# Hybrid encoder step on one core: order of loads, copies and sums around the MLP's down projection

## What is computed

```python
x = x + out                                   # attention output times w_o
h = rmsnorm(x, norm_mlp[i])
x = x + jnp.square(jax.nn.relu(h @ mlp_w_up[i])) @ mlp_w_down[i]   # hidden 4096
```

## Time and profile before

| | us |
|---|---|
| median of 3 runs | 2820.52 |
| profiled execution, device time | 2818.45 |
| its span | 2816.5 |
| PE busy | 2679.4 (95%) |
| PE weight loads busy | 2247.5 (80%) |
| DVE busy | 1735.6 (62%) |
| ACT busy | 1157.7 (41%) |
| POOL busy | 739.1 (26%) |

### The profile page before, as it was taken

One profiled execution on the slowest core, in us unless ns is written; L12 is line 12 of the kernel. 1 busy time (PEld: TensorE's weight loads), 2 busy tenths in 40 slices (PEclk: granted clock), 3 DMA queues, 4 the chain that ended last, 5 costly groups with the idle time before them and its releaser, 6 DMA issues. The chain is left out here.

```text
span 2816.5 us, 40390 instructions
## 1 busy us (share of the span) xinstructions
PE 2679.4 (95%) x14531; PEld 2247.5 (80%) x14531; DVE 1735.6 (62%) x2325; ACT 1157.7 (41%) x2260; POOL 739.1 (26%) x633
## 2 busy tenths in 40 slices
PE   7989998899999989999699999998999999999998
PEld 6878887778888878888598886776888888778886
DVE  5656665266555678888311007887485555688887
ACT  4334445243333333333312218998343333333333
POOL 3100001135544400000312115665145544300001
PEclk9999999899999999999899999999999999999999
DMA  4311113514444564533134537773324444644342
GB/s 147 87 59 46 43 52 105 187 60 145 139 135 142 186 221 132 161 128 109 62 126 146 157 109 180 173 172 113 121 91 150 135 137 141 241 159 161 123 157 101
DMA packets 285845, 368.81 MB, mean 131 GB/s; under 512 B 25952, under 2 KB 205664, under 8 KB 285664
## 3 DMA queue, kind: packets, MB, share of 16 engines
q1 hardware_dynamic: 285664, 366.42, 40.8%
HBM read 242.19 MB, written 124.16 MB: 130 GB/s over the span
## 5 line engine op out<-in xcount | busy, mean ns | idle before, releaser
L2291 DVE TENSOR_TENSOR x<-m_ps,x 128x1024 f32<-128x1024 f32 x224 | 273.1, 1219 | 98.9 <-PE m_ps L76 98.9
L2008 POOL TENSOR_TENSOR m_u<-m_u,m_u 128x512 f32<-128x512 f32 x128 | 175.8, 1384 | 340.3 <-DVE m_u L2138 335.2
L1954 POOL TENSOR_SCALAR m_stat<-m_stat 128x1 f32<-128x1 f32 x36 | 11.9, 329 | 862.2 <-ACT m_sqjunk L1901 693.8
L2126 DVE TENSOR_TENSOR m_z<-m_ps,m_part 128x512 f32<-128x512 f32 x96 | 66.3, 690 | 143.9 <-PE m_ps L76 142.0
L1759 ACT COPY m_part<-m_ps 128x512 f32<-128x512 f32 x96 | 56.4, 588 | 197.4 <-PE m_ps L76 197.4
L2114 DVE TENSOR_TENSOR m_up<-m_upr,m_up 128x512 fp32r<-128x512 f32 x128 | 87.8, 706 | 28.5 <-ACT m_up L1746 28.5
L3237 ACT ACTIVATE e_b<-e_ps 128x512 f32<-128x512 f32 (+3 forms) x192 | 95.9, 500 | 12.0 <-PE e_ps L3433 11.4
L76 PE MATMUL m_ps<-m_t1h,m_up 128*128 128x512 f32 x256 | 99.7, 390 | 0.0
L74 PE MATMUL m_ps<-m_t1h,m_up 128*128 128x512 f32 x256 | 99.6, 389 | 0.0
L75 PE MATMUL m_ps<-m_t1l,m_up 128*128 128x512 f32 x256 | 99.6, 389 | 0.0
L1746 ACT CAST m_up<-m_upr 128x512 fp32r<-128x512 f32 x128 | 75.7, 616 | 57.2 <-PE m_ps L76 57.2
(11 more groups left out here) (1175 smaller groups left out, 9093.9 us busy)
## 6 DMA issues: line engine op xcount, KB each, us to landing
scratch_u<-m_u SPq DMA_DIRECT2D x224, 256.0 KB, 2.2
m_ur<-scratch_u SPq DMA_DIRECT2D x208, 256.0 KB, 2.7
m_upr<-in_mlp_w_up SPq DMA_DIRECT2D x32, 1024.0 KB, 5.9
m_wr<-in_mlp_w_down SPq DMA_DIRECT2D x64, 512.0 KB, 6.9
scratch_x<-x SPq DMA_DIRECT2D x18, 512.0 KB, 2.6
x<-scratch_x SPq DMA_DIRECT2D x4, 2048.0 KB, 11.4
scratch_qr<-a_qrst SPq DMA_DIRECT2D x9, 512.0 KB, 3.4
a_x<-in_x_prompt SPq DMA_DIRECT2D x8, 512.0 KB, 4.9
```

The costliest lines, as they stand in the source:

```text
L2008: pool.tensor_tensor(u_st[out][:], u_st[a][:], u_st[b][:], op).then_inc(u_summed.sem, 1)
L2291: dve.tensor_tensor(out, bank[:, at:at + 2, :], out, ALU.add).then_inc(summed.sem, 1)
```

## The change

All edits are inside `output_and_mlp_stage`, for both layers. In words:

1. SP, first chunk: all seven operands of pass 0 and A11 of pass 1 are loaded in one run, then u of the last pair and the sample part of the pair before are stored, and only then comes x. x returns in five pieces (two tiles each, and the sample tile) where there were three; pieces for tiles 2, 3 and 6, 7 are issued after the weights of chunk 1. The other six operands of pass 1 are issued right after the last up product, ahead of weights "21" and "22" of chunk 1 and of the last stores; before they came after the wait for B12's low part. `load_tokens` now also waits for the low part of the buffer's last user from the ninth operand on.
2. Last up pair: ACT's third `keep_part` stands before the copies of T2, T1; DVE's second `join` and `activate` stand before the low parts of T2, T1. The sum T3 moves from POOL to DVE; T4's sum moves back behind the token parts. ACT copies S4 before B22.
3. First up pair: the weight sums S1 and S2 of pair 0 move from POOL to DVE (`first_up_sums`), between the low part of A12 and the rest of the last row tile's parts; the four pieces of T4 are copied after S2 and S1 in one run.
4. Last pass: ACT squares rows 0, 1 and the sample tile before it copies S4 and A22 of the last pass, and in layer 0 also scales two tiles before A22. POOL makes the roots of three rows before it multiplies two tiles by the gain, then two more roots, then three multiplications.

```diff
@@ SP
-                if m >= 16:
+                if m >= 8:
                     before, j = divmod(m - 8, 7)
                     sp.wait_ge(tok_lo[TOKEN_OPERANDS[j]].sem, before + 1)
...
             sp.wait_ge(up_lo.sem, UP_STEPS * PAIRS_FF)
-            load_tokens(0, "A11")
-            load_tokens(0, "A12")
-            load_tokens(0, "S2")
+            for n in TOKEN_OPERANDS:
+                load_tokens(0, n)
+            load_tokens(1, "A11")
+            store_u(LAST, 0)
+            store_sample_u(LAST - 1)
...
-                tiles = (slice(0, 4), slice(4, 8), slice(8, 9))[i]
+                tiles = (slice(0, 2), slice(2, 4), slice(4, 6), slice(6, 8), slice(8, 9))[i]
...
             sp.wait_ge(prod.sem, up_done(LAST, "P6"))
             reload_x(0)
-            store_u(LAST, 0)
-            for n in ("S1", "S3", "S4", "A22"):
-                load_tokens(0, n)
-            load_tokens(1, "A11")
             sp.wait_ge(prod.sem, up_done(LAST, "P7"))
-            reload_x(1)
             store_u(LAST, 1)
-            store_sample_u(LAST - 1)
+            reload_x(2)
             sp.wait_ge(prod.sem, up_done(LAST, "P4"))
             load_sample_tokens(0)
             store_u(LAST, 2)
             sp.wait_ge(prod.sem, up_done(LAST, "P3"))
+            for n in TOKEN_OPERANDS[1:]:
+                load_tokens(1, n)
             load_weights(1, "21")
             load_weights(1, "22")
             store_u_sums(LAST)
@@ (store_sample_u(LAST) and the wait for five low parts stay here)
             load_weights(1, "11")
             load_weights(1, "12")
-            for n in TOKEN_OPERANDS[1:]:
-                if n == "A22":
-                    sp.wait_ge(u_out[6].sem, 16 * PAIRS_FF)
-                load_tokens(1, n)
+            reload_x(1)
+            reload_x(3)
             u_stored(PAIRS_FF)
-            reload_x(2)
+            reload_x(4)
             load_sample_tokens(1)
@@ ACT, up pairs
                 if p == 0:
-                    fourth_features_hi((0, 1))
                     up_operand_hi("S2", 0)
                     up_operand_hi("S1", 0)
-                    fourth_features_hi((2, 3))
+                    fourth_features_hi((0, 1, 2, 3))
...
-                if not more:
-                    weight_hi(0, "T2")
-                    weight_hi(0, "T1")
...
                 keep_part(p, 2)
...
                 if not more:
-                    weight_hi(0, "T3")
+                    weight_hi(0, "T2")
+                    weight_hi(0, "T1")
                     token_hi(0, "A11")
...
                 else:
+                    weight_hi(0, "T3")
                     token_hi(0, "A12")
                     token_hi(0, "S2")
...
             copy_sample(PAIRS_FF - 1)
+            token_hi(0, "S4")
             weight_hi(0, "B22")
-            token_hi(0, "S4")
@@ ACT, last pass
+            for i in range(3):
+                squares_2(i)
+            token_hi(LAST_G, "S4")
             if final:
-                for i in range(NT):
+                token_hi(LAST_G, "A22")
+                for i in range(3, NT):
                     squares_2(i)
             else:
-                for i in range(3):
-                    squares_2(i)
                 scale_early(0)
                 scale_early(1)
+                token_hi(LAST_G, "A22")
                 squares_2(3)
@@ POOL
-            up_sums(0, ("S1", "S2"))
             inverse_rms(NPT, stat, squared, mean, rs)
             up_sums(0, ("S3", "S4"))
...
-            pool.wait_ge(*weight_in(0, "22"))
-            pool.wait_ge(prod.sem, up_done(PAIRS_FF - 1, "P5"))
-            pool.tensor_tensor(sum_t3[:], wt_raw[0]["22"][:], wt_raw[0]["12"][:], ALU.subtract).then_inc(
-                wt_sum["T3"].sem, 1)
             u_sums(PAIRS_FF - 1)
...
             for i in range(NT):
                 inverse_rms(i, stat_2, squared_2, mean_2, rs_2)
-                if i in POOL_SCALES:
-                    if i == 0:
-                        pool.wait_ge(gain_2_in.sem, 16)
-                    pool.wait_ge(scaled_2.sem, i + 1)
-                    pool.tensor_tensor(yn[i][:], yn[i][:], gain_2[:], ALU.mult).then_inc(normed_pool.sem, 1)
+                if POOL_SCALES and i in (2, 4):
+                    for early in (0, 1) if i == 2 else (2, 3, 4):
+                        apply_gain(early)
@@ DVE, first pair (then S2, S1, scale, four pieces of T4)
                     up_operand_lo("A12", 0)
+                    first_up_sums()
                     features_lo(t - 1, (2, 3))
@@ DVE, last pair
                     weight_lo(0, "B21")
                     weight_sum(0, "T1")
                     weight_sum(0, "T2")
-                    weight_lo(0, "T2")
-                    weight_lo(0, "T1")
...
                 join(p, 1)
                 activate(p, 1)
...
-                    weight_lo(0, "T3")
-                    weight_sum(0, "T4")
+                    weight_sum(0, "T3")
+                    weight_lo(0, "T2")
+                    weight_lo(0, "T1")
                     token_lo(0, "A11")
                 activate_sample(p)
...
                 else:
+                    weight_lo(0, "T3")
                     token_lo(0, "A12")
                     token_lo(0, "S2")
...
                     token_lo(0, "S1")
                     token_lo(0, "S3")
+                    weight_sum(0, "T4")
```

More of the change, by code:

```diff
@@ L1363, in output_and_mlp_stage @@
         u_summed, wt_sum = signal("usum"), {n: signal(f"wsum{n}") for n in ("T1", "T2", "T3", "T4")}
-        x_back = [signal(f"xb{i}") for i in range(3)]
+        x_back = [signal(f"xb{i}") for i in range(5)]
         down, summed, sample_summed = signal("down"), signal("acc"), signal("acc8")
@@ L1667, in _ @@
                     load_weights(c, q)
-                if c >= 2:
-                    for hp in range(2):
-                        for n in TOKEN_OPERANDS:
-                            if 2 * c + hp >= 4:
-                                load_tokens(2 * c + hp, n)
+                for g in (2 * c, 2 * c + 1):
+                    for n in TOKEN_OPERANDS if g >= 4 else ():
+                        load_tokens(g, n)
             if not final:
@@ L1882, in _ @@
                 weight_hi(c, "T4")
-                for n in ("A12", "S2", "S1", "S3", "S4"):
+                for n in ("A12", "S2", "S1", "S3"):
                     token_hi(g + 1, n)
+                if not more:
+                    continue
+                token_hi(g + 1, "S4")
                 token_hi(g + 1, "A22")
-                if more:
-                    for n, b in (("", "B11"), ("A11", "B21"), ("A12", "T2"), ("S2", "T1"), ("S1", "T3"), ("S3", "B22"),
-                                 ("S4", "")):
-                        if n:
-                            token_hi(g + 2, n)
-                        if b:
-                            weight_hi(c + 1, b)
+                weight_hi(c + 1, "B11")
+                for n, b in (("A11", "B21"), ("A12", "T2"), ("S2", "T1"), ("S1", "T3"), ("S3", "B22")):
+                    token_hi(g + 2, n)
+                    weight_hi(c + 1, b)
+                token_hi(g + 2, "S4")
             def squares_2(i):
@@ L2110, in _, with first_up_sums @@
             dve.wait_ge(gain_in.sem, 16)
+            def first_up_sums():
+                dve.wait_ge(up_in[0].sem, 16)
+                dve.wait_ge(out_done.sem, HALVES * NT)
+                dve.tensor_tensor(up_sum["S1"][:], up_source("A21", 0), up_source("A22", 0), ALU.add).then_inc(
+                    up_summed.sem, 1)
+                dve.wait_ge(up_summed.sem, 1)
+                dve.tensor_tensor(up_sum["S2"][:], up_source("S1", 0), up_source("A11", 0), ALU.subtract).then_inc(
+                    up_summed.sem, 1)
             def up_operand_lo(n, p):
@@ L2230, in _ @@
                 if p == 0:
[L2231 removed]
                     up_operand_lo("S2", 0)
+                    up_operand_lo("S1", 0)
                     scale(NT - 1)
[L2234 to L2235 removed]
+                    fourth_features_lo((0, 1, 2, 3))
                     for n in ("S3", "A21", "A22"):
@@ L2286, in accumulate @@
                 if g < 2:
-                    dve.wait_ge(x_back[rows].sem, 16)
+                    dve.wait_ge(x_back[2 * rows + hp].sem, 16)
                 after(dve, summed, added_at(g, n) - 1)
```

26 lines of the change are left out of this document (15 added, 11 removed).

## The result

The changed kernel takes 2791.32 us (median of four runs, 2790.07 to 2794.74) against 2820.05 of the kernel before on the same chip (2819.43 to 2820.55): 28.7 us less, ratio 0.990, 95% interval 0.9883 to 0.9917. The forecast was 2787.0 with a range of 2774 to 2801. The profiled execution after took 2794.74 us, the slowest of the four. The kernel before, measured again beside each set of experiments, had medians of 2819.74 to 2820.11 us, so the times of different sets may be held against each other.

The account below looks back on a forecast made before the run. PE is busy 2679 of 2816.5 us, so only its idle or slow time can be won. Transition 14.5, tail 16.0 and first up pair 3.0 make 33.5 us: 2818.45 becomes 2785.0, median 2787.0; range 2774 to 2801.

Parts of the forecast that it names:

- tail of layer 0: Last pass of layer 0: waits before the first and third transposes go, 16.0 us gained, bounds 4 to 16.5.
- first up pair, both layers: P6's wait for S2's low part goes, then DVE's list sets the sample product; 3.0 us gained, bounds -2.4 to 6.
- transition, both layers: From up to down pass: 8.0 us gained in layer 0 and 6.5 in layer 1, sum 14.5.
- The rival in which the third wait stays: Tail of layer 0: third transpose still waits, only 4 to 8 of 16 us are won, 2797; chance 0.10.
- Step 1: Transition of layer 0: the 3.52 us wait before the last up pair's P4 goes; ACT's third PSUM copy needs P7 alone.
- step 5: Transition of layer 0: the 6.55 us wait before the down P3 goes; A12 of pass 1 has landed by 993.
- Step 2: Transition of layer 0: DVE's last activation ends at 989.3, before 991.8; taken as 2.5 us earlier.
- Step 3: Transition, gate of B12: queue drained at about 999.4; down P7 starts at 1003.5 to 1005.5, taken as 1004.3, before 1005.46.
- DMA is later still: Rival: B12's store stands behind more loads, P7 at 1007.5 or worse, 14.5 us becomes 5, 2796.5; chance 0.17.
- The operand of s0: Sample operand for the down pass's sample product: landed near 988.5, wanted at 989.6; P7's wait swallows 1 us of lateness.
- The rule on shared ports: DVE instructions with both inputs in SBUF and POOL instructions exclude each other; four of each were taken to cost 1.7 us.
- The strict reading: POOL's four sums end 2.9 us later, P7 at 1005.5 or a little more; the sum about 2 us smaller.

Follow-up runs that it names:

- experiment 2: Changed kernel with half of the last-pass order taken back: GpSimd's order alone 2800.69 us, ScalarE's order alone 2797.36 us.
- experiments 1 to 3: Changed kernel with parts taken back: whole last-pass tail order 2808.04 us, GpSimd's order there alone 2800.69, ScalarE's alone 2797.36, first up pair 2794.08.
- Experiment 7: Changed kernel with the loads of pass 1's remaining token operands put back behind the wait for B12's low part: 2799.46 us.
- Experiment 9: Changed kernel with all of x issued in the two early places, 2048 KB each instead of 1024 KB: 2799.71 us.
- experiment 6: Changed kernel with pass 0's two loads of the sample's operands issued ahead of x piece 2: 2791.94 us.

## Why the forecast held, and where a size was off

The time lies 4.3 us above the forecast of 2787.0. The order of the waits and their releasers came out as forecast; P7's waits of 5.96 and 5.71 us lie just under the 6 to 8 named, and B12's copy came 13.5 and 14.9 us behind the last activation, not 10 to 12. The terms of the sum, forecast and measured between the traces from P1:

| | forecast | traces | by undoing it |
|---|---|---|---|
| tail of layer 0 | 16.0 | 15.8 | 16.7 |
| first up pair, both layers | 3.0 | 2.2 | 2.8 |
| transition, both layers | 14.5 | 9.4 | (in parts) |
| sum | 33.5 | 27.4 | |

- **Tail.** Right. Four groups and four products from P6's end to the fifth group took 1348.23 - 1333.75 = 14.5 us, the upper end of the 14.1 to 14.5 forecast. Undoing it brings 16.7 us back by the medians and 14.5 by the trace of the tail. The rival in which the third wait stays is what GpSimd's old order does alone (experiment 2), at 9.4 us.
- **First up pair.** Right in kind: DVE's list sets the sample product. Of the 1.36 us seen in layer 1, undoing the part brings back 0.84; that the rest is owed to it is not shown.
- **Step 1** (wait before the last P4 gone) and **step 5** (wait before P3 gone; x and weights in time) are right. Behind P7 the transition gained 17.2 - 10.6 = 6.6 us in layer 0 and 15.95 - 10.38 = 5.6 in layer 1, which is what the forecast had (8.0 and 6.5, each less the 1.2 us that P7 was to come sooner). The 5 us that are missing all lie ahead of P7.
- **Step 2** (last activation 2.5 us sooner) holds in layer 0: 3.2, and 2.4 without what the first pair gave. In layer 1 it is 2.7, and 1.3 without the first pair's 1.36: T1's sum waits 3.06 us for its load there instead of 2.18 and, by the same count, comes 1 us later. I had carried layer 0's number over without looking at layer 1's queue.
- **Step 3 is the mis-sized term.** P7 was to start 1.2 us sooner per layer; net of the first pair it starts 0.2 us later in layer 0 and 2.6 later in layer 1. The sums' contention came as forecast (1.7 us; measured 6.94 - 5.27 = 1.67, and the store's issue 1.8 later behind the activation). The landing didn't: I had the queue drained 1.3 us sooner, since 0.5 MB less passed through the whole stretch. From the store's issue to B12's copy it took 0.8 us longer in layer 0 and 2.2 in layer 1. In the two layers of five builds (the changed kernel and those of experiments 1 to 3) it took 4.5 to 6.2 us, 5.3 in the mean, against the 4.0 of the one trace before.

  The landing times of layer 0 show where the 1.3 us went. Each 2 MB piece of x had held the queue for 5.1 us and each 1 MB piece now holds it for 2.5, but the six token loads hold it for 4.3, so the swap saved 0.8. And S1, S3, S4 and A22 of pass 0 with A11 of pass 1 land over 4.6 us where it had been 3.7; before they stood behind x, now ahead of it, and why that is slower is open.

  Experiment 7 takes the six loads away, and the landing is 2.6 to 2.7 us shorter. Experiment 9 issues 2 MB of x more ahead of the six: the store, itself issued 4.2 and 3.0 us later, still lands 1.7 and 1.3 us later behind its issue. So what was issued just ahead and what was issued long before both count while the queue stays full, and one rate for all bytes doesn't price them. The Trainium skill (DMA: Bandwidth & Descriptors, "Queues, rings and completion order") says that each DMA engine takes its descriptors in ring order; the landings between 993 and 1004 us agree but for one small piece (the store issued at 998.80 lands at 1002.71, the one issued at 998.44 at 1003.39).

  The rival "DMA is later still" was thus partly true; both layers together lost 5 of the 9.5 us that it priced.
- **The operand of s0** was to be the closest call, 1 us. It was late by 1.64 and 2.82 us (0.57 to 2.12 in the other builds), and P7's wait swallowed it, as said: experiment 6 removes it and the time stays.
- **The rule on shared ports.** Rows first: in the trace beside POOL's four sums stand three DVE instructions with two SBUF inputs (low parts of S4, A22, B22), and the fourth that I had counted, A11's, starts 0.1 us before the sums end. POOL took 1.67 us longer; DVE paid as well, 1.64 us for S4's low part and 2.31 for B22's where such instructions take 0.68 and 1.22. Singly, each waits for the other's end: POOL's first sum ends at 992.74 and S4's low part at 993.28; the second sum, begun at 992.81, ends at 994.44 (1.63 us instead of 1.29); B22's low part, begun at 994.94, runs on 1.08 us from the third sum's end at 996.17; and the fourth sum takes 2.29 us and ends 1.16 behind that low part. The addition to x between them, with one input in PSUM, takes its usual 1.21. The Trainium skill (SBUF — State Buffer, "Who interferes with whom") says that the shared port pair is an exclusive lock and that the order of issue decides who blocks. The rows agree: the bill is split between the two. That my 4 x 0.43 us gave the right total is luck in part: the four sums took between 1.26 and 2.29 us. The strict reading, POOL paying all 2.9 us, was wrong.

Left open: why pass 0's operands land more slowly ahead of x than behind it, and 1.3 us of difference between the medians and the sum of the terms, of which 0.3 lie between the fifth transpose group of layer 0 and P1 of layer 1. The 1.5 us by which the store landed later behind its issue in layer 1 than in layer 0 are no fixed difference: in the four builds that leave the stage as it is they are 1.3, 0.9, 0.1 and -0.6, and in experiment 6 both layers take 5.1.

## To carry to other kernels

When loads are moved ahead, list for every store or load that something waits for what will have been issued just before it, and price its landing by that, from the landing times of such transfers; a lower total over the stretch alone did not bring it sooner here. Read a merged row of issues singly: it can hold a wait. Follow a gate link by link (last producer, issue, landing, copy, consumer) in each layer of its own, and ask of every instruction in an in-order list whether it has to stand in front of what waits behind it: here two copies, two low parts, one small store and one pair of loads, moved by a few places, were worth 16.7 us, more than the whole transition had given. Small roots ahead of long multiplications on one engine, and squares as soon as their row is complete, are cheap edits that show only where another engine waits for the end of that chain.

## What the runs showed of the hardware

Issuing a DMA is not of constant cost. The six loads of 256 KB took SP 0.36 to 0.53 us each to issue in layer 0 of the changed kernel, 2.71 together. With 2 MB more issued ahead of them (experiment 9) they took 7.44 us, and 7.95 in layer 1, where one of them took 4.09. So a full queue delays what stands behind on SP twice, at its issue and at its landing: from the issue of the 128 KB store to the copy that waits for it, it is 4.7 and 6.2 us in the two layers of the changed kernel, 6.4 and 7.6 with those 2 MB.
In experiment 7, with fewer loads just ahead, it was 2.0 and 3.6.

A GpSimd sum of 128x512 takes 1.29 us alone, and beside DVE instructions with two inputs in SBUF the two take turns, instruction by instruction (1.63 and 2.29 us for a sum, 1.64 for a DVE low part of 0.68).
